# Transformer block pair on one core: wide operands for the second mixing's 24 gate blocks, padded and merged small products

## The reference, cut to what matters

```python
# first block, stick-breaking attention: masked logits of 8 heads
mask = key_pos[None, :] < t[:, None]
a = jnp.where(mask, jnp.exp(jax.nn.log_sigmoid(z) + suffix), 0.0)
# first block, sparse attention: the compressed branch (15 compressed keys)
o_c = jnp.einsum('bhgqc,bchd->bqhgd', p_c.astype(v_cmp.dtype), v_cmp)
# second block, spatial gating: 8 groups of mixing weights and a bias per token
mixed = jnp.einsum('gts,bcsgd->bctgd', w, v) + b_s.T[None, None, :, :, None]
# second block, gates of the three branches
gates = jax.nn.sigmoid(z[..., COL_GATE:] + b_gate[l]).reshape(B, S, N_BRANCH, D_MODEL)
merged = (gates[:, :, 0] * (y_a @ w_branch_a[l]) + gates[:, :, 1] * (y_b @ w_branch_b[l])
          + gates[:, :, 2] * (y_c @ w_branch_c[l]))
```

## Time and profile before

| | |
|---|---|
| median of 3 runs | 1105.55 us |
| the profiled execution, its own time | 1106.11 us |
| its span | 1104.4 us |
| TensorE busy | 1076.5 us (97%) |
| VectorE busy | 795.8 us (72%) |
| ScalarE busy | 615.2 us (56%) |
| mean granted TensorE clock | 0.997 of full |

### The profile page before, as it was taken

How to read it: one execution, slowest core, us unless ns; L and a number is a source line. 1 busy time by engine, 2 the same in 40 slices (tenths; PEclk the granted TensorE clock), 3 DMA queues, 4 the chain that set the end, 5 groups by cost and what they waited for, 6 DMA issues and landing times.

```text
span 1104.4 us, 19438 instructions
## 1 busy us (share of the span) xinstructions
PE 1076.5 (97%) x7182; PEld 977.9 (89%) x7182; DVE 795.8 (72%) x1371; ACT 615.2 (56%) x1127; POOL 52.8 (5%) x83
## 2 busy tenths in 40 slices
PE   5899999999999999999999999999999999999998
PEld 3699998899899998888888888999999998888887
DVE  4777778866698865559888655665876878888853
ACT  2575656655555544556565545688645357555532
POOL 3012110000010000000000000000000002000000
PEclk9999999999999999999999999999999999999999
DMA  9979763346576566666666664555444555666663
GB/s 355 319 264 358 256 210 114 108 148 182 173 273 203 179 187 188 182 183 191 190 190 191 189 190 138 155 151 163 126 131 117 153 172 172 191 191 191 190 189 116
DMA packets 58507, 208.96 MB, mean 189 GB/s; under 512 B 7055, under 2 KB 8591, under 8 KB 57912
## 3 DMA queue, kind: packets, MB, share of 16 engines
q1 hardware_dynamic: 51320, 180.00, 53.3%
q0 software_dynamic: 7104, 27.81, 6.9%
HBM read 204.62 MB, written 3.16 MB: 188 GB/s over the span
## 4 chain that ended last, share of the span: by engine, by line
PE 89%; DVE 4%; ACT 3%; DMA 3%; issue 1%; SPq 1%; DVEq 0%; ACTq 0%
PE bank L645 88%; DMA ring<-in_stream 3%; DVE ring_rounded L1705 1%; ACT rounded_rounded L1284 1%; PE bank L915 1%; ACT body L1460 1%; SPq L600 0%; ACT body_rounded L1333 0%; DVE ada_acc L1775 0%; DVE body_rounded L1749 0%; DVE part L2268 0%; DVE x L2039 0%; ACT body L1476 0%; DVE u_rounded L2105 0%; DVE u L1834 0%
## 5 line engine op out<-in xcount | busy, mean ns | idle before, releaser
L645 PE MATMUL bank<-u_rounded,rounded_rounded 128*128 128x256 f32 (+1 forms) x2368 | 553.6, 318 | 3.8 <-ACT u_rounded L1333 2.2
L1705 DVE TENSOR_TENSOR ring_rounded<-ring,rounded_rounded 128x1024 fp32r<-128x1024 f32 x326 | 396.6, 1222 | 159.2 <-ACT rounded_rounded L1284 153.2
L645 PEld LDWEIGHTS bank<-u_rounded,rounded_rounded 128*128 128x128 f32 x2368 | 393.6, 191 | 40.9 <-issue 6.2
L645 PE MATMUL bank<-u_rounded,ring_rounded 128*128 128x256 f32 x1528 | 429.1, 281 | 0.0
L1284 ACT ACTIVATE rounded_rounded<-ring 128x1024 fp32r<-128x1024 f32 x326 | 343.0, 1055 | 131.2 <-PE bank L645 105.7
L645 PE MATMUL bank<-body_rounded,rounded_rounded 128*128 128x256 f32 (+1 forms) x1248 | 336.4, 339 | 1.2 <-DVE body_rounded L2010 1.2
L645 PEld LDWEIGHTS bank<-u_rounded,ring_rounded 128*128 128x128 f32 x1528 | 291.2, 191 | 0.1
L645 PE MATMUL bank<-body_rounded,ring_rounded 128*128 128x256 f32 x928 | 260.4, 281 | 0.0
L645 PEld LDWEIGHTS bank<-body_rounded,rounded_rounded 128*128 128x128 f32 x1248 | 216.2, 190 | 29.3 <-DVE body_rounded L2010 1.6
L645 PEld LDWEIGHTS bank<-body_rounded,ring_rounded 128*128 128x128 f32 x928 | 176.0, 190 | 0.0
L1239 POOL TENSOR_TENSOR turned<-turned 128x256 f32<-128x256 f32 x20 | 18.1, 903 | 629.7 <-ACT turned L1536 397.3
(11 more groups left out here) (278 smaller groups left out, 988.9 us busy)
## 6 DMA issues: line engine op xcount, KB each, us to landing
ring<-in_stream SPq DMA_DIRECT2D x328, 512.0 KB, 3.6
ada_ring<-in_ada POOLq DMA_DIRECT2D x35, 512.0 KB, 6.0
body<-in_ada SPq DMA_DIRECT2D x7, 512.0 KB, 14.9
body<-in_ada POOLq DMA_DIRECT2D x4, 512.0 KB, 16.9
mem_parts_kept<-body_rounded POOLq DMA_DIRECT2D x2, 1024.0 KB, 8.3
body_rounded<-mem_parts_kept POOLq DMA_DIRECT2D x2, 1024.0 KB, 6.9
x<-in_x_t SPq DMA_DIRECT2D x2, 512.0 KB, 6.8
body<-in_mem_t SPq DMA_DIRECT2D x2, 512.0 KB, 11.3
```

Source lines behind the costliest of these rows:

```text
L645: return nc.tensor.matmul(out, lhs, rhs, start=start, stop=stop, skip_group_check=True)
L1705: v.tensor_tensor(R(w), w, R(slot_round(q)), ALU.subtract).then_inc(slot_split, 1)
```

## The change

1. All 24 gate blocks are projected with `project_wide`. ScalarE copies columns 256 to 511 of the bank to the gate's tile (`copy_gate_half`); VectorE adds columns 0 to 255 to it, and this frees the bank (`add_gate_half`); ScalarE takes the tanh in place later, by a list TANH_AT: in step i of the loop those of the gates projected a step earlier, and of gate i for i below 4 (`gate_tanh_of`). VectorE adds gates 0 to 3 in the loop over the key heads, and the other twenty at the beginning of steps 0 to 9 of its loop, ahead of `logits(i+1)`.
2. The two mask products of `sb_logits` become one rounded matmul of 256 columns, with the mask read twice and the two diagonal blocks written. ScalarE rounds the identity and the mask once, after the last query norm.
3. The product over 15 compressed keys and that over one bias row take all 128 rows; the rows beyond are cleared by GpSimd (one memset more at the start, one of 128x1024 ahead of the bias load, with a wait).

```diff
+TANH_AT = [([2 * i + 2, 2 * i + 3] if 0 < i < 11 else []) + ([i] if i < 4 else []) for i in range(12)]
...
+        mats = sb_split("mats", [P, len(MATRICES), P])
+        ident_rounded = sb("ident_rounded", [P, P], F32R)
...
+        lines = sb("lines", [P, 1024])
+        vcmp = lines[:, 0:256].rearrange("p (s c) -> p s c", s=2)
+        turned_c = turned[:, :, :, 384:512]
...
-                mm(ps[:, 0:P], mat("ident"), mat("not_before"))
-                mm(ps[:, T:T + P], mat("ident"), mat("not_before"), stop=True).then_inc(sb_logits_ready, 1)
+                if h == 0:
+                    pe.wait_ge(mask_rounded, 2)
+                diagonal = ps[:, :].rearrange("p (b t) -> p b t", t=P)[:, 0::2, :]
+                masks = R(mat("not_before")).unsqueeze(1).to_broadcast([P, 2, P])
+                mm(diagonal, ident_rounded[:, :], masks, stop=True).then_inc(sb_logits_ready, 1)
...
-                ins = mm(ps[:, 0:T], vcmp[0:N_CMP, s, :], turned_c[0:N_CMP, i % 2, :, :], stop=s == 1)
+                ins = mm(ps[:, 0:T], vcmp[:, s, :], turned_c[:, i % 2, :, :], stop=s == 1)
...
-                project(f"gate{b}", KD, u_parts)
+                project_wide(f"gate{b}", KD, u_parts)
...
-                done(mm(ps[:, 0:T], mats[0:1, MAT["ones"], :], sg_b[:, b * T:(b + 1) * T], stop=True), name)
+                done(mm(ps[:, 0:T], mat("ones"), lines[:, b * T:(b + 1) * T], stop=True), name)
...
-                    project(f"gate{2 * i + RAW_GATES}", KD, u_parts)
-                    project(f"gate{2 * i + RAW_GATES + 1}", KD, u_parts)
+                    project_wide(f"gate{2 * i + RAW_GATES}", KD, u_parts)
+                    project_wide(f"gate{2 * i + RAW_GATES + 1}", KD, u_parts)
...
-            for t in (vcat[:], pair_v[:], kcat[:], pair_k):
+            for t in (vcat[:], pair_v[:], kcat[:], pair_k, turned_c[:, 1, :, :]):
...
+            pool.memset(lines[:, :], 0.0).then_inc(lines_cleared, 1)
+            pool.wait_ge(lines_cleared, 1)
             pool.dma_start(sg_b, sg_b_d).then_inc(loaded["sg"], 16)
...
+            a(ident_rounded[:, :], mat("ident"), ACT.Copy).then_inc(mask_rounded, 1)
+            a(R(mat("not_before")), mat("not_before"), ACT.Copy).then_inc(mask_rounded, 1)
...
+            def copy_gate_half(g):
+                output(f"gate{g}")
+                a(gates[:, g, :], bank(f"gate{g}")[:, T:2 * T], ACT.Copy).then_inc(gate_copied, 1)
+            def gate_tanh_of(g):
+                taken(f"gate{g}")
+                a(gates[:, g, :], gates[:, g, :], ACT.Tanh, scale=0.5, bias=half_bias[:, g:g + 1]).then_inc(gate_ready, 1)
...
             for b in range(RAW_GATES):
-                copy(gates[:, b, :], f"gate{b}")
+                copy_gate_half(b)
...
-                    two_gates(2 * i + RAW_GATES)
-                if i < RAW_GATES:
-                    taken(f"gate{i}")
-                    a(gates[:, i, :], gates[:, i, :], ACT.Tanh, scale=0.5, bias=half_bias[:, i:i + 1]).then_inc(raw_gate_ready, 1)
+                    copy_gate_half(2 * i + RAW_GATES)
+                    copy_gate_half(2 * i + RAW_GATES + 1)
+                for g in TANH_AT[i]:
+                    gate_tanh_of(g)
...
+            def add_gate_half(g):
+                output(f"gate{g}")
+                dve.wait_ge(gate_copied, g + 1)
+                free(v.tensor_tensor(gates[:, g, :], bank(f"gate{g}")[:, 0:T], gates[:, g, :], ALU.add), f"gate{g}")
             for h in range(8):
+                if h % 2 == 0:
+                    add_gate_half(h // 2)
...
             def gate_branch(dst, g, name, reach=True):
+                dve.wait_ge(gate_ready, 1 + [n for at_i in TANH_AT for n in at_i].index(g))
...
             for i in range(12):
+                if i < 10:
+                    add_gate_half(2 * i + RAW_GATES)
+                    add_gate_half(2 * i + RAW_GATES + 1)
```

More of the change, by code:

```diff
@@ L375, in build @@
         mod = sb("mod", [P, 48])
-        mats = sb("mats", [P, len(MATRICES), P])
+        mats = sb_split("mats", [P, len(MATRICES), P])
+        ident_rounded = sb("ident_rounded", [P, P], F32R)
         cols = sb("cols", [P, N_COLS])
@@ L418, in build @@
         bias_cmp = sb("bias_cmp", [P, 8, TT, N_CMP])
-        lines = sb("lines", [33, 1024])
-        buckets, bias_line, sg_b = lines[:, 0:512], lines[0:8, 512:1024], lines[0:1, :]
-        vcmp = lines[0:16, 0:256].rearrange("p (s c) -> p s c", s=2)
+        lines = sb("lines", [P, 1024])
+        buckets, bias_line, sg_b = lines[0:33, 0:512], lines[0:8, 512:1024], lines[0:1, :]
+        vcmp = lines[:, 0:256].rearrange("p (s c) -> p s c", s=2)
         table = sb("table", [33, 8])
@@ L437, in build @@
         turned = sb("turned", [P, 2, 2, 512])
-        turned_c = turned[0:16, :, :, 384:512]
+        turned_c = turned[:, :, :, 384:512]
         kc_ext = turned[:, :, :, :].rearrange("p a b c -> p (a b c)")[:, 0:4 * (T + 32)].rearrange("p (w h t) -> p w h t", w=2, h=2)
@@ L494, in halves_before @@
             return 0 if before == KF else 2 * KF2 - 1
+        mask_rounded = sem("mask_rounded")
+        lines_cleared = sem("lines_cleared")
         hidden_raw, hidden_rounded, hidden_ready = sem("hidden_raw"), sem("hidden_rounded"), sem("hidden_ready")
@@ L501, in build @@
         branches_added = sem("branches_added")
-        gelu_ready, raw_gate_ready = sem("gelu_ready"), sem("raw_gate_ready")
+        gelu_ready, gate_ready, gate_copied = sem("gelu_ready"), sem("gate_ready"), sem("gate_copied")
         ones_ready = sem("ones_ready")
@@ L1369, in _ @@
                 a(R(u[:, i, :]), u_lo[:, i, :], ACT.Identity, bias=mod[:, i:i + 1]).then_inc(u_rounded, 1)
-            act.wait_ge(zeros_ready, 4)
+            act.wait_ge(zeros_ready, 5)
             for t in range(TT):
@@ L1397, in _ @@
             inv_rms("qa3", HD, lambda: taken("qa1"))
+            act.wait_ge(loaded["mats"], 16)
+            a(ident_rounded[:, :], mat("ident"), ACT.Copy).then_inc(mask_rounded, 1)
+            a(R(mat("not_before")), mat("not_before"), ACT.Copy).then_inc(mask_rounded, 1)
             for b in range(4):
@@ L1442, in _ @@
                     ps = bank("cmp_out_v")
-                    act.wait_ge(zeros_ready, 5)
+                    act.wait_ge(zeros_ready, 6)
                     a(vcmp[0:N_CMP, 0, 0:HD], ps[0:N_CMP, 0:HD], ACT.Copy)
@@ L1658, in _ @@
             act.wait_ge(half_bias_ready, 1)
[L1660 to L1663, removed]
             attend(0)
@@ L1862, in _ @@
             free(v.tensor_copy(bias_line, bank("bias")[0:8, :]), "bias")
-            dve.wait_ge(zeros_ready, 4)
+            dve.wait_ge(zeros_ready, 5)
             for n, off in (("ks", 0), ("kw", P)):
```

## The result

The changed kernel took 1110.31 us (median of 21 executions, 1106.06 to 1116.1), the kernel before 1107.2 beside it (21 executions, 1105.05 to 1110.68). The ratio is 1.0028, 95% interval 1.0017 to 1.004: 3.1 us slower. A second measurement, with 12 and 24 executions, gave 1.0033 (1.0016 to 1.005). The forecast was 1105.1, in a range of 1101.0 to 1109.0; the time lies above it. 1.65 us of that distance is the starting point, since the median of three that was shown (1105.55) is lower than that of 21. The rest is the change: +3.1 where -0.5 was expected.

A forecast was written before the change was run, and what follows sets the result against it. TensorE, busy 97% of the span, was taken as the bound. Gains 2.5 + 2.0 + 1.0 + 3.1 = 8.6, losses 6.4 + 1.7 = 8.1: -0.5 from 1106.1 gives 1105.6, as a median 1105.1 us, range 1101.0 to 1109.0.

The forecast's parts named there:

- The masks: Mask products of the stick-breaking heads: one rounded matmul saves 0.33 us a head, six of eight heads count, 2.0 us gained.
- The 15-row product: Product over compressed keys in the sparse heads: full rows save 0.28 us each, waits swallow most, 1.0 us gained.
- The one-row product: Bias-row product beside the spatial products: full rows remove 0.39 us extra, eight times, 3.1 us gained.
- The pause: At gate7, TensorE waits once for VectorE's add of gate4, which stands behind sg_norm: 6.4 us lost.
- A: Rival: gate7 doesn't wait, or VectorE reaches gate4's add in time; no lower clock; 1097.0 us, chance 0.08.
- B: Rival: padding the few-row products earns nothing, so their 4.1 us fall away; 1109.2 us, chance 0.10.
- D: Rival: clock stays full or the wait at gate7 starts late, values' gain comes whole; 1102.1 us, chance 0.12.
- the gates: All 24 gate projections: 192 wide chunks at 0.347 instead of 0.360 us each, 2.5 us gained.
- nothing is counted: VectorE's adds (10 us) and ScalarE's copies and tanhs (about 8 us) cost TensorE nothing; 4 us if uncovered.
- two tanhs of 0.5 fit in: In a later step ScalarE waits 1.55 us for VectorE's logits, from 814.2, room for two 0.5 us tanhs.
- rival C: VectorE stays late behind the wait at gate7, so gate9 or next ones wait 1 to 4 us; 1107.6, chance 0.10.
- the clock: Behind the wait at gate7, one stretch of 3.4 us at 1.2 instead of 2.4 GHz: 1.7 us lost.

The follow-up runs named there:

- pads_only: The kernel before with the padded 15-row and one-row products alone: 1104.94 us, ratio 0.9974.
- wide_only: The kernel before with the wide gate blocks, their copies, adds and tanhs alone: 1117.23 us, ratio 1.0074, in six executions.
- after: First traced execution of the changed kernel, no further edit: 1106.06 us, the quickest of its 21.
- early: The changed kernel with VectorE's adds of gate4 and gate5 moved ahead of logits(1): 1104.98 us, ratio 0.9962.
- adds_mid: The changed kernel with VectorE's adds of gate4 and gate5 between attend_scale(1) and sg_norm: 1108.29 us, ratio 1.0008.

## Why the prediction was wrong

**Right.** The masks: -2.0 forecast, -1.98 measured (121 to 195), with the given-back part where it was put. The 15-row product: -1.0, -0.93, all of it behind 205 us and nothing in the heads ahead, where 0.2 was forecast. The one-row product: -3.1, -3.14. The pause: 6.4, 6.0, once, at `gate7`, for the reason given. Rivals A and B fell, and D: the clock was low at the pause in all five traces. Rival B was also what the Trainium skill (TensorE: Matmul & The Clock Gate, "Why this matters for your kernels") gives with its K=32 as slow as K=128; pads_only measures 4.05 us against it, so the measurement decides, for plain products among other work.

**Wrong, the gates.** The step is "192 x 0.0133 = 2.5 us", the rate of the wide SwiGLU, and with it "nothing is counted" for VectorE's and ScalarE's new work. In the traces of the changed kernel the blocks earned 0.18 (gates 0 to 3), nearly nothing up to 787, and 4.52 - 3.14 = 1.38 in the steps, and paid 0.88 at 855 us: 0.7 us net. Two reasons show. The gates 0 to 3 and the first steps run at 0.3533 a chunk, not 0.3467 (see the last section); against 0.360 that is half the gain. In wide_only, without padded products, nearly all blocks up to 848 us run at 0.353, and they earn 0.71 there. And between 848 and 862 every kernel with the wide blocks loses 0.87 to 0.89 us and none with narrow ones does; 0.62 of it is TensorE's wait for VectorE's L2290. The traces show what is ahead of L2290. ScalarE and VectorE after, then before:

```profile
852.30 0.90 ACT L1637 ACTIVATE body<-body,half_bias 128x256 f32<-128x256 f32 x2
853.10 2.00 ACT L1293 ACTIVATE rounded_rounded<-ring 128x1024 fp32r<-128x1024 f32 x2
854.24 1.23 DVE L1722 TENSOR_TENSOR ring_rounded<-ring,rounded_rounded 128x1024 fp32r<-128x1024 f32 x1 [1.51 <-ACT rounded_rounded L1293]
855.39 0.75 DVE L2290 SCALAR_TENSOR_TENSOR body<-body,bank 128x256 f32<-128x256 f32 x2
```
```profile
853.01 0.58 ACT L1346 ACTIVATE turned<-bank 128x512 f32<-128x512 f32 x1
853.49 1.05 ACT L1284 ACTIVATE rounded_rounded<-ring 128x1024 fp32r<-128x1024 f32 x1
854.64 1.22 DVE L1705 TENSOR_TENSOR ring_rounded<-ring,rounded_rounded 128x1024 fp32r<-128x1024 f32 x1 [0.71 <-ACT rounded_rounded L1284]
855.79 0.74 DVE L2268 SCALAR_TENSOR_TENSOR body<-body,bank 128x256 f32<-128x256 f32 x2
```

After, ScalarE takes the tanhs of the last two gates (step 10 of TANH_AT) between the copy of the turned weights (L1355, at 851.82) and the rounding of a slot. VectorE waits for that rounding (1.51 us in all ten traces with wide gates, 0.71 in all six with narrow ones), splits the slot, and only then gates the branch. From the copy to the rounding 1.28 us pass instead of 0.48, and from the copy to the gating 3.57 instead of 2.78. So it is ScalarE's new work that costs this time, against "two tanhs of 0.5 fit in", which the earlier trace rows gave for an earlier step. No run moved the two tanhs. It is a small rival C, at the end of the steps and by another engine than it named. Without the pause the blocks even cost time: early from 690 to 862, less the 3.13 of the pads, is -2.42 + 3.13 = +0.7 us, its wait at `gate9` with it.

**Wrong, the clock.** The step is "I expect one such stretch: +1.7". The stretch that gave this price, behind the wait in the earlier trace rows, cost nothing itself: after has none there and loses nothing by comparison (last section). At the pause itself the size was nearly right: from 756 to 787 the seven traces with it gain 7.71 to 8.72, mean 8.16; adds_mid gains 2.13 with 2.2 of pause and full clock, so 5.9 of it is pause and 2.2 clock. What the step left out is that another edit would cost clock at another place. The mask product takes work out of the heads just ahead of a wait of TensorE that grows from 1.80 to 2.44 us, and there and at 300 us low clock appears. The four long ones took 1.8 to 2.2, three took another 1.5 at 302 to 307 us: 12.7 us in ten traces, 1.3 on average. That the masks bring it is shown by the four pairs of kernels taken together and 6 traces in 10 against 0 in 6; that it is the longer wait, and not the one rounded matmul in place of plain ones, is only argued.

**The sum again.** -2.0 - 0.9 - 3.1 - 0.7 + 5.9 + 2.2 + 1.3 = +2.7 us. The two measurements gave +3.1 and +3.7, with about 1.3 and 1.9 us to either side. Of the 3.2 us between -0.5 and +2.7, the gates have 1.8 and the clock 1.8; the shorter pause and the other terms take 0.4 back. The sum leaves out the slow pace behind 905 us, 3.4 us in half of the traces with wide gates: the kernel before seems to have it too (last section). If wide gates bring it more often, which no run settles, they cost up to 1.7 us more.

## What to carry to other kernels

Where two large terms cancel, the small ones decide. A gain of 13 ns on a step of 360 is soon lost when the freeing of a buffer moves to a busier engine: find the place of that engine's new instruction in its program order first (here the two lines of early, worth 6.5 us of mean span). Then look at what the other engines' new instructions stand in front of, at the end of the loop too, and ask whether the edit is still wanted (here it isn't: masks and pads alone are quickest). Price each edit in the mean over executions and not from one trace: the masks save 2.0 us in the traces and 0.7 in the mean. Few-row plain products among full ones are worth padding here: 4 us for two memsets and wider slices.

## What the runs showed of the hardware

The wide chunks (one rounded matmul of 512 and one of 256 columns) have two paces at the same full granted clock: 0.3467 and 0.3533 us each, the same over hundreds of chunks (distances of starts repeat as 347, 347, 346 ns in one stretch of the kernel before and as 361, 349, 350 in another). The pace changed only where a wait or other matmuls came between. In all 16 traces it is 0.3533 up to about 490 us and 0.3467 from there to 676. Behind 905 us it differs between executions, 0.3533 in five of the ten traces with wide gates and in none of the six with narrow ones, and costs 3.4 us. The kernel before seems to have both as well: its seven executions at a mean clock of 1.000 took 1104.7, 1105.4, 1105.8 and then 1108.5, 1108.7, 1108.9, 1109.2 us. What sets the pace wasn't found.

Low clock came in stretches of 3.41, 6.83 or 10.24 us (and cut short at the end of the kernel), and its price depends on what lies in it. The stretch at 676 us costs nothing, being in a chain of waits: after has none there and its shift stays at -4.28. One of 6.83 us in the heads costs some 2, one of 3.41 us at 307 us, where TensorE is busy throughout, 1.5.
